# Stick-breaking attention and selected attention in one phase, and where the top-k search runs

## The reference, cut to what matters

```
IDX_HEADS, TOPK = 8, 128                     # n_top = min(256, 512 // 4)

def dsa_mixer(...):                          # "selected attention"
    rel   = relu(einsum(q_idx, k_idx))       # 8 small index heads
    score = where(k_pos <= q_pos, sum_h w_idx * rel, NEG_INF)
    idx   = top_k(score, 128)                # the search
    p     = masked_softmax(q @ k[idx], idx <= q_pos)
    return p @ v[idx]

def stick_breaking_mixer(q, k, v):
    z      = q @ k * scale                   # mask: k_pos < q_pos
    log_1m = where(mask, log_sigmoid(-z), 0)
    after  = reverse_cumsum(log_1m) - log_1m
    a      = where(mask, exp(log_sigmoid(z) + after), 0)
    return a @ v
```

## Time and profile before

| | |
|---|---|
| median of 3 runs | 3432.64 us (3432.55 to 3441.43) |
| profiled execution | 3431.76 us, its span 3430.0 us |
| PE busy | 3276.2 us, 96% |
| PEld busy | 2630.2 us, 77% |
| DVE busy | 1550.5 us, 45% |
| ACT busy | 1289.9 us, 38% |
| POOL busy | 331.2 us, 10% |
| mean granted TensorE clock | 0.987 |

### The profile page before, as it was taken

How to read it: one execution, slowest core, us unless ns; L and a number is a source line. 1 busy time by engine, 2 the same in 40 slices (tenths; PEclk the granted TensorE clock), 3 DMA queues, 4 the chain that set the end, 5 groups by cost and what they waited for, 6 DMA issues and landing times. The chain is left out here.

```text
span 3430.0 us, 37430 instructions
## 1 busy us (share of the span) xinstructions
PE 3276.2 (96%) x14880; PEld 2630.2 (77%) x14880; DVE 1550.5 (45%) x2443; ACT 1289.9 (38%) x2234; POOL 331.2 (10%) x156
## 2 busy tenths in 40 slices
PE   7999999999999999999889999999999988899998
PEld 6867678878888888877666788878887767678886
DVE  4154522244343333446975433443334488663333
ACT  3344642333232322234665422242223446642222
POOL 0411324400000000014000000000000330000000
PEclk9999999999999999999999999999999999999999
DMA  4311223323333333322001233323332310023332
GB/s 145 92 43 44 86 62 105 99 80 101 96 99 98 98 94 98 98 99 90 13 1 62 86 99 98 94 85 98 97 94 101 105 50 1 19 80 98 97 94 74
DMA packets 77069, 280.60 MB, mean 82 GB/s; under 512 B 8800, under 2 KB 9056, under 8 KB 76640
## 3 DMA queue, kind: packets, MB, share of 16 engines
q1 hardware_dynamic: 76896, 278.21, 25.9%
HBM read 276.08 MB, written 2.10 MB: 81 GB/s over the span
## 5 line engine op out<-in xcount | busy, mean ns | idle before, releaser
L539 ACT ACTIVATE w_hi<-raw_slabs 128x1024 fp32r<-128x1024 f32 x496 | 524.5, 1058 | 1285.4 <-PE ps L579 1132.6
L554 DVE TENSOR_TENSOR w_lo<-raw_slabs,w_hi 128x1024 fp32r<-128x1024 f32 x372 | 454.9, 1223 | 747.7 <-ACT w_hi L539 747.5
L579 PE MATMUL ps<-in_hi,w_hi 128*128 128x512 f32 x1840 | 719.8, 391 | 9.6 <-DVE in_lo L902 7.7
L579 PE MATMUL ps<-in_lo,w_hi 128*128 128x512 f32 x1840 | 717.4, 390 | 0.0
L579 PE MATMUL ps<-in_hi,w_lo 128*128 128x512 f32 x1840 | 717.3, 390 | 0.0
L579 PE MATMUL ps<-parts,w_hi 128*128 128x512 f32 x2240 | 691.5, 390 | 0.9 <-DVE scratch L1480 0.8
L554 POOL TENSOR_TENSOR w_lo<-raw_slabs,w_hi 128x1024 fp32r<-128x1024 f32 x124 | 307.1, 2479 | 2472.9 <-ACT w_hi L539 2472.9
L579 PEld LDWEIGHTS ps<-parts,w_hi 128*128 128x128 f32 x2240 | 420.3, 188 | 90.8 <-issue 1.9
L579 PE MATMUL ps<-parts,w_lo 128*128 128x512 f32 x1120 | 435.8, 389 | 0.0
L579 PEld LDWEIGHTS ps<-in_hi,w_hi 128*128 128x128 f32 x1840 | 346.1, 188 | 87.3 <-issue 8.7
L579 PEld LDWEIGHTS ps<-in_hi,w_lo 128*128 128x128 f32 x1840 | 346.4, 188 | 72.4
(11 more groups left out here) (277 smaller groups left out, 3491.7 us busy)
## 6 DMA issues: line engine op xcount, KB each, us to landing
raw_slabs<-weights SPq DMA_DIRECT2D x510, 512.0 KB, 3.6
big<-rope SPq DMA_DIRECT2D x2, 2304.0 KB, 8.9
x_resid<-xT SPq DMA_DIRECT2D x8, 256.0 KB, 4.6
outT<-x_resid SPq DMA_DIRECT2D x8, 256.0 KB, 2.0
const_cols<-consts SPq DMA_DIRECT2D x1, 836.0 KB, 9.1
scratch<-brow SPq DMA_DIRECT2D x1, 768.0 KB, 9.9
vector_cols<-vec SPq DMA_DIRECT2D x2, 45.5 KB, 9.6
vector_cols<-vec SPq DMA_DIRECT2D x1, 69.0 KB, 3.3
```

The source lines that it names most:

```text
L539: self.nc.scalar.activation(self.w_hi[:, m % SPLIT, :], self.raw[:, n % RAW, :], ACT.Copy)\
L554: (self.nc.gpsimd if i is None else self.nc.vector).tensor_tensor(self.w_lo[:, m % SPLIT, :], self.raw[:, n % RAW, :], self.w_hi[:, m % SP ...
L579: mm = k.nc.tensor.matmul(out, lhsT, rhs, start=(c == 0 and m == 0), stop=(last and m == 2))
```

## The change

`stick_phase` is replaced by `two_branch_phase`, which takes a unit of stick-breaking attention and a unit of selected attention in each round, and the second short `attention_phase` is gone. The selected units use their own buffers in `big` (rows 25 to 30, which held queries and keys of the joined attention). PSUM is dealt out anew: three banks for the stick scores instead of four, one for the selected scores instead of three, and one each for the two kinds of transposes and the two kinds of results. The search has to be finished before this phase, so the steps are cut anew: 0 to 11 in the projections, 12 to 47 in the joined attention, none in the merged phase. Six semaphores of the first block are used again under new names (`spare`), since the new phase needs more of them. No instruction of the computation is added or taken away; DMAs and weights are untouched.

```diff
-TOP_CUTS = (TOP_STEPS, 32, 44)
+TOP_CUTS = (12, 32, TOP_STEPS * (QB - 1))
...
-    STEPS = {**{j: 1 for j in range(12, 16)}, 16: 2, 17: 5, 18: 5}
+    STEPS = {13: 1, 14: 1, 15: 1, 16: 1, 17: 4, 18: 4}
...
     attention_phase(k, units, select, range(TOP_CUTS[0], TOP_CUTS[2]))
...
-    stick_phase(k, units, select, range(TOP_CUTS[2], TOP_STEPS * (QB - 1)))
...
-    attention_phase(k, units)
+    two_branch_phase(k, sticks, picks)
...
+        k.spare = ["stabil", "u_turned", "u_col", "max_laid", "em_row", "em_laid"]
```

The new function, without its blank lines:

```diff
+def two_branch_phase(k, sticks, picks):
+    nc = k.nc
+    scored, soft, logged, broken, rest, exponent, probs_ready, turned, laid, unit_done, stored = [
+        k.flag(n) for n in ("scored", "soft", "logged", "broken", "rest", "exponent", "probs_ready",
+                              "turned", "laid", "unit_done", "stored")]
+    row_max, expd, row_inv, p_scored, p_ready, p_turned, p_laid, p_done, p_stored = [
+        k.flag(n) for n in ("row_max", "probs_expd", "row_inv", "pick_scored", "pick_ready", "pick_turned", "pick_laid",
+                              "pick_done", "pick_stored")]
+    n = len(sticks)
+    z = lambda i: k.ps[:, i % 3, 0:sticks[i].width]
+    soft_at, rest_at, laid_at, probs = [lambda i, b=b: k.scr[:, b + i % 3, :] for b in (0, 3, 6, 9)]
+    p_probs, p_laid_at = [lambda i, b=b: k.big[:, b + i % 3, :] for b in (25, 28)]
+    p_score = lambda i: k.ps[:, 3, 0:picks[i].width]
+    col = lambda kind, i: k.stat[:, kind, i:i + 1]
+    assert len(picks) == n and all(u.first and u.last for u in sticks + picks)
+    with k.block() as block:
+        @block.tensor
+        def _(pe):
+            for i in range(n + 5):
+                if i < n:
+                    if i >= 3:
+                        pe.wait_ge(probs_ready, k.at(probs_ready, i - 2))
+                    score(k, sticks[i], i % 3).then_inc(scored, 1)
+                    if i >= 1:
+                        pe.wait_ge(expd, k.at(expd, i))
+                    score(k, picks[i], 3).then_inc(p_scored, 1)
+                if 0 <= i - 2 < n:
+                    u = i - 2
+                    pe.wait_ge(rest, k.at(rest, u + 1))
+                    nc.tensor.matmul(z(u), k.c("ident"), rest_at(u)[:, 0:sticks[u].width], start=False, stop=True,
+                                     skip_group_check=True)\
+                        .then_inc(exponent, 1)
+                if 0 <= i - 3 < n:
+                    u = i - 3
+                    pe.wait_ge(probs_ready, k.at(probs_ready, u + 1))
+                    if u >= 1:
+                        pe.wait_ge(laid, k.at(laid, u))
+                    turn(k, sticks[u], probs(u), 4).then_inc(turned, 1)
+                if 0 <= i - 1 < n:
+                    u = i - 1
+                    pe.wait_ge(p_ready, k.at(p_ready, u + 1))
+                    if u >= 1:
+                        pe.wait_ge(p_laid, k.at(p_laid, u))
+                    turn(k, picks[u], p_probs(u), 5).then_inc(p_turned, 1)
+                if 0 <= i - 4 < n:
+                    u = i - 4
+                    pe.wait_ge(laid, k.at(laid, u + 1))
+                    if u >= 1:
+                        pe.wait_ge(stored, k.at(stored, u))
+                    weigh(k, sticks[u], laid_at(u), 6).then_inc(unit_done, 1)
+                if 0 <= i - 2 < n:
+                    u = i - 2
+                    pe.wait_ge(p_laid, k.at(p_laid, u + 1))
+                    if u >= 1:
+                        pe.wait_ge(p_stored, k.at(p_stored, u))
+                    weigh(k, picks[u], p_laid_at(u), 7).then_inc(p_done, 1)
+        @block.scalar
+        def _(act):
+            def lay_pick(u):
+                cols = picks[u].width
+                act.wait_ge(p_turned, k.at(p_turned, u + 1))
+                if u >= 3:
+                    act.wait_ge(p_done, k.at(p_done, u - 2))
+                nc.scalar.activation(p_laid_at(u)[:, 0:cols], k.ps[:, 5, 0:cols], ACT.Copy).then_inc(p_laid, 1)
+            def store(u, one, done, bank, signal):
+                lo, hi = one.rows
+                act.wait_ge(done, k.at(done, u + 1))
+                nc.scalar.activation(one.out, k.ps[lo:hi, bank, 0:P], ACT.Copy).then_inc(signal, 1)
+            k.use_table(EXP_LN)
+            for i in range(n + 6):
+                l = soft_at(i)[:, 0:sticks[i].width] if i < n else None
+                if 0 <= i - 2 < n:
+                    lay_pick(i - 2)
+                if i < n:
+                    act.wait_ge(scored, k.at(scored, i + 1))
+                    if i >= 3:
+                        act.wait_ge(rest, k.at(rest, i - 2))
+                    nc.scalar.activation(l, z(i), ACT.Abs).then_inc(soft, 1)
+                if 0 <= i - 5 < n:
+                    store(i - 5, sticks[i - 5], unit_done, 6, stored)
+                if i < n:
+                    act.wait_ge(soft, k.at(soft, 2 * i + 1))
+                    nc.scalar.activation(l, l, ACT.Exp, scale=-1.0).then_inc(soft, 1)
+                if 0 <= i - 3 < n:
+                    store(i - 3, picks[i - 3], p_done, 7, p_stored)
+                if i < n:
+                    act.wait_ge(soft, k.at(soft, 2 * i + 2))
+                    nc.scalar.activation(l, l, ACT.Ln, bias=1.0).then_inc(logged, 1)
+                    w = picks[i].width
+                    act.wait_ge(row_max, k.at(row_max, i + 1))
+                    if i >= 3:
+                        act.wait_ge(p_turned, k.at(p_turned, i - 2))
+                    nc.scalar.activation(p_probs(i)[:, 0:w], p_score(i), ACT.Exp, bias=col(0, i), scale=1.0,
+                                         accum_out=col(1, i)).then_inc(expd, 1)
+                if 0 <= i - 2 < n:
+                    u = i - 2
+                    act.wait_ge(exponent, k.at(exponent, u + 1))
+                    if u >= 3:
+                        act.wait_ge(turned, k.at(turned, u - 2))
+                    nc.scalar.activation(probs(u)[:, 0:sticks[u].width], z(u), ACT.Exp).then_inc(probs_ready, 1)
+        @block.vector
+        def _(dve):
+            for i in range(n + 4):
+                if i < n:
+                    dve.wait_ge(p_scored, k.at(p_scored, i + 1))
+                    nc.vector.tensor_reduce(col(0, i), p_score(i), AX, ALU.max, negate=True).then_inc(row_max, 1)
+                if 0 <= i - 3 < n:
+                    u = i - 3
+                    cols = sticks[u].width
+                    dve.wait_ge(turned, k.at(turned, u + 1))
+                    if u >= 3:
+                        dve.wait_ge(unit_done, k.at(unit_done, u - 2))
+                    nc.vector.tensor_copy(laid_at(u)[:, 0:cols], k.ps[:, 4, 0:cols]).then_inc(laid, 1)
+                if i < n:
+                    w = sticks[i].width
+                    l, r = soft_at(i)[:, 0:w], rest_at(i)[:, 0:w]
+                    dve.wait_ge(logged, k.at(logged, i + 1))
+                    nc.vector.scalar_tensor_tensor(l, z(i), 0.0, l, ALU.max, ALU.add).then_inc(broken, 1)
+                    if i >= 3:
+                        dve.wait_ge(exponent, k.at(exponent, i - 2))
+                    dve.wait_ge(broken, k.at(broken, i + 1))
+                    nc.vector.tensor_tensor_scan(r[:, ::-1], k.c("one").broadcast_to([P, w]), l[:, ::-1], 0.0,
+                                                 ALU.mult, ALU.subtract).then_inc(rest, 1)
+                    p, inv = p_probs(i)[:, 0:picks[i].width], col(1, i)
+                    dve.wait_ge(expd, k.at(expd, i + 1))
+                    nc.vector.reciprocal(inv, inv).then_inc(row_inv, 1)
+                    dve.wait_ge(row_inv, k.at(row_inv, i + 1))
+                    nc.vector.tensor_scalar(p, p, inv, None, ALU.mult).then_inc(p_ready, 1)
+    k.passed(scored=n, soft=2 * n, logged=n, broken=n, rest=n, exponent=n, probs_ready=n, turned=n, laid=n, unit_done=n,
+             stored=n, row_max=n, probs_expd=n, row_inv=n, pick_scored=n, pick_ready=n, pick_turned=n, pick_laid=n,
+             pick_done=n, pick_stored=n)
```

More of the change, by code:

```diff
@@ L364, in __init__ @@
         self.flags = {}
+        self.spare = []
         self.base = {}
@@ L406, in flag @@
     def flag(self, name):
+        if name not in self.flags and self.spare:
+            old = self.spare.pop()
+            self.flags[name], self.base[name] = self.flags.pop(old), self.base.pop(old)
         if name not in self.flags:
@@ L1957, in attention_phase @@
              select_made=rows_done(steps))
-def stick_phase(k, units, index, steps):
+def two_branch_phase(k, sticks, picks):
     nc = k.nc
@@ L1974, in _ @@
         def _(pe):
-            for i in range(n + 4):
+            for i in range(n + 5):
                 if i < n:
-                    if i >= 4:
-                        pe.wait_ge(probs_ready, k.at(probs_ready, i - 3))
-                    score(k, units[i], i % 4).then_inc(scored, 1)
+                    if i >= 3:
[4 more added lines that the diff above has]
+                    score(k, picks[i], 3).then_inc(p_scored, 1)
                 if 0 <= i - 2 < n:
```

(7 more changed lines are left out.)

40 lines of the change are left out of this document (2 added, 38 removed).

## The result

| | kernel before | changed kernel |
|---|---|---|
| median of 20 runs each | 3434.86 us | 3440.62 us |
| lowest, highest | 3431.42, 3449.04 | 3435.67, 3450.39 |
| profiled execution, its span | 3431.76, 3430.0 | 3435.67, 3433.9 |

The ratio is 1.0018, with a 95% interval of 1.0011 to 1.0025. 1.0018 is inside the 0.3% and 3440.62 us inside the predicted range, but it is a loss of some 6 us (3.9 between the profiled spans) where the sum said + 0.8. The profiled execution of the changed kernel is the fastest of its twenty, 4.95 us under their median; that of the kernel before is 3.1 us under its own.

The account below looks back on a forecast made before the run. DVE was taken to bound the joined attention, PE the selected attention, no engine the stick phase. - 2.3 + 8.4 - 5.7 = + 0.4 us a layer, + 0.8 for both, gave 3433 us, range 3421 to 3444.

Parts of the forecast that it names:

- Projections, - 2.3: End of the projections: DVE loses two steps and a mask, 2.3 us a layer; 2.6 by the skill's rule.
- Joined attention, + 8.4: Joined attention: eight more steps and two masks on DVE cost 9.8 us, 1.4 hidden in its waits.
- Merged phase, - 5.7: Merged phase: PE's work of 52.8 us plus waits gives 62.1 us, against 67.8 for the two stages before.
- (c): Middle of the merged phase: scores wait for ACT's last Exp three units earlier; 0.5 us for four rounds, 2.0 in all.
- I don't expect that: Merged phase: TensorE's clock, 1.00 in both later stages before, was not expected to fall.
- Start and end, 3.5 + 3.8: Merged phase: waits of 3.5 us until the first units fill it and 3.8 us while the last unit runs alone.
- the slow rival: Merged phase: single PSUM banks make rounds wait, 0.6 us each; phase 69.7 us, kernel 3449 us; chance 0.13.
- The sign on `laid` and `stored`: Merged phase: no wait for either of these two semaphores should be over 0.3 us.
- No difference: Whole kernel: merging gains about what the longer search costs, time within 0.3%, 3425 to 3442 us; chance 0.71.
- Slower, by the single banks: Merged phase: PE waits until single PSUM banks are emptied, 0.6 us a round, + 8 us a layer, 3449 us; chance 0.13.
- Faster, by PE: Merged phase: PE needs only its weight loads' 46.2 us, not 52.8; - 6.2 us a layer, 3420 us; chance 0.07.
- Faster, by the search: Joined attention: steps hide in DVE's 7.0 us of gaps, growth 2.8 to 4; - 5.2 us a layer, 3422 us; chance 0.09.

Follow-up runs that it names:

- e11: Kernel before, its two phases kept, with only the four search steps of the stick phase moved into the joined attention: 3437.03 us, ratio 1.0004.
- e1: Kernel before with the changed cut of the search alone, stick phase and selected attention still two phases: 3442.92 us, ratio 1.0023.
- e9: Changed kernel with only the odd heads' stores moved from ScalarE to VectorE: 3439.99 us in one execution.
- e6: Changed kernel with the merged phase taking the heads in the order 0, 2, 1, 3: 3440.32 us in one execution.
- e7: Changed kernel with 16 search steps kept in the projections and the stick units' last Exp ahead of the selected units' Exp: 3430.56 us, ratio 0.9982.
- e2: Changed kernel with the projections keeping their 16 search steps and 32 in the joined attention: 3433.61 us, ratio 1.0001.
- e12: e7 with the stores of the odd heads alone moved from ScalarE to VectorE: 3431.37 us, ratio 0.9983.
- e3: Changed kernel with both ScalarE stores moved from between Abs, Exp and Ln to behind the last Exp: 3462.77 us, ratio 1.0079.

## Why the prediction was nearly right, by its own steps

*Projections, - 2.3.* Measured - 2.9 and - 2.3. DVE did end this block, and the collision moved as the rule of the Trainium skill (SBUF — State Buffer, Who interferes with whom) says: of DVE's two-input instructions the one that met POOL's L558 was now L711 with 2.12 us, and L714, 2.72 before, took 0.69. The trace agrees with it. Its 2.6 came nearer to the first layer's 2.9 than 2.3 did; in the second layer the L711 that was caught took 2.79, as long as the L710 set free (2.80 before), and 2.3 was right. PE's idle time at the boundary did not stay at 4 to 6: it fell to 3.1 and 1.5, as DVE left PE less to wait for.

*Joined attention, + 8.4.* Measured + 7.4 and + 6.6. The working gave the four steps of 512 with their mask 6.05 us and the four of 256 with theirs 3.8, less 1.4 hidden. They measured 3.0 and 4.3 (e11, e1): half of the wide steps hid, nothing of the narrow ones, which cost 0.5 more than they were priced at. The sum is off by 1.0 and 1.8 us in the profiled execution, the fastest one. Over the fourteen layers of the merged kernels with 36 steps the mean is + 7.9 (+ 6.6 to + 9.9), so the sum was right to half a microsecond there, by two errors of its parts against each other.

*Merged phase, - 5.7.* This is the step that failed: - 2.8 and - 2.4. The phase was to take 62.1 us and took 65.0 (65.35 in the second layer). PE's own work was the term mis-sized: 14.1 us for four rounds instead of 13.2, so 56.3 instead of 52.8. The waits, put at 9.3, were 65.0 - 56.3 = 8.7; that they came out near is luck, since what made them was not what the prediction named. Four things in it:
First, "the four steps taken from the stick phase leave no time there" was wrong. It does not enter the 62.1, but it gives the gain a wrong source: by e11 2.7 us come from taking these steps out, though no engine was full, and they are as much as the whole gain of the changed kernel. They stood in VectorE's queue, in a phase of chains across three engines; that they were in the way there is argued, that the time went with them is shown. The merging itself is worth 1.0.
Second, PE's own work. e9's turn 2 shows no wait of PE and lasts 14.08 us, e6's 14.09, and no turn 2 or 3 of any run is shorter, where 13.2 was worked out. PE's timeline of e9 has the weighings of a selected unit of four blocks and of one block, each with the next score:

```profile
1780.86 1.06 PE L1851 MATMUL ps<-big 128*128 128x128 f32 x8
1781.76 0.81 PE L1836 MATMUL ps<-big 128*128 128x384 f32 x2
...
1784.58 0.39 PE L1851 MATMUL ps<-big 128*128 128x128 f32 x2
1785.07 1.13 PE L1836 MATMUL ps<-big 128*128 128x512 f32 x2
```

In the selected attention of the kernel before they read so:

```profile
1802.65 1.05 PE L1847 MATMUL ps<-scratch,big 128*128 128x128 f32 x8
1803.46 0.48 PE L1832 MATMUL ps<-parts,in_hi 128*128 128x256 f32 x2
...
1804.24 0.39 PE L1847 MATMUL ps<-scratch,big 128*128 128x128 f32 x2
1804.38 0.59 PE L1832 MATMUL ps<-parts,in_hi 128*128 128x384 f32 x2
```

From start to start that is 0.90 and 0.49 us, before 0.81 and 0.14. Over a turn the weighings of the selected units take 2.67 us where they took 1.90, which is 0.77 of the 0.88; 0.44 of it stand before the scores of two of the four rounds and may be waits too short for the view to name. The stick units' scores take 2.61, not 2.30: the prediction scaled the narrow ones from the widest. The rest of the rows take 0.2 us less than worked out.
Third, (c), the middle's 0.5 us for four rounds. ScalarE's end of the round was picked as the loop that matters, but without the stores. Those of the odd heads add 0.3 us each, serial, and the phase 1.7 to 1.9 (e9). And the selected units' Exp of up to 0.69 us stands in front of the last Exp, for which PE waits at the head of each turn: some 2 us (e7 against e2).
Fourth, the clock, "I don't expect that": it was at its lower level at the start, 1.0 us by e2.
Start and end, 3.5 + 3.8, were costed too high and hid these last two: e12, without them, has less than that for all its waits. With the clock and the order mended, e7 takes 64.1 and 64.5 us where the sum gives 62.1 + 2.25 = 64.4; with the odd stores off ScalarE e12 takes 63.4. So e12 leaves 63.4 - 2.25 - 4 x 14.08 = 4.8 us for all waits, not 9.3.
One more slip in the working changes nothing above: the slow rival's 69.7 us at 0.6 us a round replaces the 2.0 us of (c), and its 67 us at 0.3 a round adds to them; counted alike, 0.3 a round gives 64.9.
*The signs.* In the joined attention DVE waits 1.2 us, and PE is busy for 60.1 of 65.0 us in the merged phase (92%): these signs came as written. Rounds 13.7 us apart did not. The sign on `laid` and `stored` failed in one place, the last weighing of the phase:

```profile
PE ps L1851 <- ACT act L2038: 0.5, 1, 0.5
```

*The rivals.* "No difference" came true, at its slow edge. "Slower, by the single banks" was not it: the banks bind only when the stores come late, as e3 shows (+ 12 us in the phase). "Faster, by PE" needed a turn shorter than PE's rows from start to start; none was, and the turns were longer. In e9's turn 2 PE's rows follow each other for 14.08 us without a wait that the view shows, while its weight loads were busy 11.6, 82%. Read as the prediction read it, as time to be won, the rule of the Trainium skill (Perfetto Trace Analysis, Identifying the Most-Contended Engine) on LDWEIGHTS busy time leaves 18% there. No run here won it with these float32 matmuls; whether other matmuls could is not shown. "Faster, by the search" failed on the second four steps, 4.3 us.

*The balance.* Moving four steps from the projections to the joined attention gains 2.3 to 2.9 us and costs 4.3, and with it comes the clock's 1.0: + 2.4 to 3.0 us a layer, 5 to 6 in all, with the 4.3 of e1. That is e2's distance to the changed kernel (1.0001 against 1.0018), and why the change as made lost. The profiled spans differ by 3.9 us, the two layers' stretches by 3.6; that these are so near is partly chance, since 1.6 us came back between them and 1.4 were added behind the second, where nothing is changed. The medians differ by 5.8. The joined attention can be the rest: it took 103.26 and 102.48 us in the profiled execution and 103.7 in the mean of the fourteen layers, 1.7 us more for both layers together. No slower execution of the changed kernel itself was profiled, so this stays an estimate. That the ratio fell inside the range owes something to luck: three terms were off, by - 0.6, - 1.0 and + 2.9 us in the first layer, and partly cancelled.

## What to carry to other kernels

When two phases are merged, walk each in-order queue for a whole round, small copies included, and put first what the engine that is to be full waits for; here the order of two Exps was worth more than the merging. Undo a combined change part by part: the gain here lay in taking a search out of a chain (2.7 us, which the joined attention took back with 3.0), and the loss in adding four more steps to a stage whose engine was already full, neither in the headline.
A single bank is fine while its emptying stands early in the reader's queue; where tidying up moves it late, it costs a wait in every round.

## What the runs showed of the hardware that was not expected

ScalarE's small copies of 64 x 128 to lanes 0 to 63 overlap their neighbours (1.21 us from Abs to the pick's Exp, with two of them or with none, 1.19), and those to lanes 64 to 127 do not (1.88). The copies are alike otherwise: the same two PSUM banks, the same size, 0.26 and 0.27 us of their own. Each reads the lanes that it writes.

The granted clock fell to its lower level in the first 8 us of the merged phase in 11 of 14 layers of the seven merged kernels whose joined attention has 36 steps, and in none of 8 layers of the four merged kernels that have 32. PE's busy share in the last 20 us ahead of it was much the same: 15.2 us in the changed kernel's first layer (part of it at the lower clock), 15.4 in e2, 16.1 before. e1, with 36 steps and two phases, kept 1.00 in both layers, though its code up to there is that of the changed kernel. The joined attention has it too: in its last 20 us the mean clock was 0.91 or 0.92 in 11 of the 16 layers with 36 steps and 1.00 in all 12 with 28 or 32. So the 36 steps go with it but don't decide it alone, and what does is open.
